# Moving the last group of a modulation map from layer 0's retention stage to layer 1's attention stage

## What is computed

```
for layer 0 and layer 1:
    m = silu(cond) @ w_mod[layer] + b_mod[layer]        # 6 x 1024 columns: shift, scale, gate of two sub-layers
    h = x * (1 + scale) + shift
    layer 0:  out = [latent attention(h), bidirectional retention(h)] @ w_out
    layer 1:  out = windowed attention(h) @ w_out       # 16 heads in 4 groups of keys
    x = LayerNorm(ALPHA * x + gate * out)
    x = LayerNorm(ALPHA * x + gate2 * MoE(x * (1 + scale2) + shift2))   # 64 experts, top 8
```

## Time and profile before

| what | us |
|---|---|
| median of three runs | 1731.41 |
| lowest and highest run | 1728.42, 1732.64 |
| span of the profiled execution | 1731.9 |
| layer 0's retention, start of the block to `product(0, 0)` | 211.8 to 260.7 |
| layer 1's attention, start of the block to the next block's first matmul | 990.3 to 1054.2 |
| PE busy over the span | 1548.0 (89%) |
| DVE, ACT, POOL busy | 587.6, 351.9, 239.1 |
| chain that ended last: PE, DMA, all other engines | 20%, 13%, under 4% |
| moved by DMA | 586.76 MB, mean 339 GB/s |

### The profile page before, as it was taken

How to read it: one execution, slowest core, us unless ns; L and a number is a source line. 1 busy time by engine, 2 the same in 40 slices (tenths; PEclk the granted TensorE clock), 3 DMA queues, 4 the chain that set the end, 5 groups by cost and what they waited for, 6 DMA issues and landing times. The chain is left out here.

```text
span 1731.9 us, 19203 instructions
## 1 busy us (share of the span) xinstructions
PE 1548.0 (89%) x6862; PEld 737.9 (43%) x6862; DVE 587.6 (34%) x1428; ACT 351.9 (20%) x768; POOL 239.1 (14%) x223
## 2 busy tenths in 40 slices
PE   4899889997799899999889889998699899999987
PEld 1566644542344334344334744543244344344332
DVE  2233685532123111111137675632133111111117
ACT  3224621211011111111114272211011111111120
POOL 0010111111011123211100000111011122211100
PEclk9999999998899999999999989998899999999998
DMA  9890389599999999999994116699999999999994
GB/s 383 346 359 34 136 334 360 211 421 421 398 411 420 409 373 410 399 413 420 378 410 154 41 41 246 260 382 420 404 392 420 410 387 395 395 408 413 391 375 172
DMA packets 112498, 586.76 MB, mean 339 GB/s; under 512 B 22154, under 2 KB 24618, under 8 KB 54160
## 3 DMA queue, kind: packets, MB, share of 16 engines
q1 hardware_dynamic: 89264, 533.84, 76.1%
q0 software_dynamic: 22560, 50.00, 7.5%
q10 hardware_dynamic: 576, 1.66, 0.3%
HBM read 570.99 MB, written 45.30 MB: 356 GB/s over the span
## 5 line engine op out<-in xcount | busy, mean ns | idle before, releaser
L3021 DVE TENSOR_TENSOR scratch<-scratch,bank 128x256 f32<-128x256 f32 x84 | 51.5, 613 | 584.7 <-ACT scratch L2989 556.2
L2896 PE MATMUL bank<-weights,scratch 128*64 128x512 f32 x384 | 181.0, 625 | 49.4 <-DMA scratch<-in_moe_w_up 45.4
L2896 PE MATMUL bank<-scratch 128*64 128x512 f32 x352 | 169.1, 636 | 35.1 <-DMA weights<-in_moe_w_up 23.3
L2897 PE MATMUL bank<-scratch 128*64 128x512 f32 x384 | 187.8, 646 | 0.0
L2897 PE MATMUL bank<-weights,scratch 128*64 128x512 f32 x384 | 178.7, 619 | 0.0
L2989 ACT ACTIVATE scratch<-bank 128x256 f32<-128x256 f32 x84 | 32.2, 383 | 643.9 <-PE bank L2897 425.9
L2896 PEld LDWEIGHTS bank<-weights,scratch 128*64 128x64 f32 x384 | 53.4, 144 | 164.1 <-issue 163.9
L2896 PEld LDWEIGHTS bank<-scratch 128*64 128x64 f32 x352 | 50.1, 147 | 143.0 <-issue 142.8
L2626 POOL DMA_INDIRECT y_rows<-hP,y_idx x39 | 41.5, 1063 | 452.6 <-ACT hP L2997 328.7
L2902 PE MATMUL bank<-weights,scratch 128*128 128x512 f32 x224 | 98.5, 593 | 1.7 <-DMA weights<-in_moe_w_up 1.7
L2611 POOL DMA_INDIRECT hP<-h_rows,tok_idx x78 | 81.4, 1043 | 129.1 <-PE bank L2572 61.7
(11 more groups left out here) (402 smaller groups left out, 2405.6 us busy)
## 6 DMA issues: line engine op xcount, KB each, us to landing
weights<-in_moe_w_gate SPq DMA_DIRECT2D x62, 1024.0 KB, 12.9
weights<-in_moe_w_up SPq DMA_DIRECT2D x62, 1024.0 KB, 20.1
weights<-in_moe_w_down SPq DMA_DIRECT2D x62, 1024.0 KB, 20.7
scratch<-in_moe_w_gate SPq DMA_DIRECT2D x60, 1024.0 KB, 12.8
scratch<-in_moe_w_up SPq DMA_DIRECT2D x60, 1024.0 KB, 21.6
scratch<-in_moe_w_down SPq DMA_DIRECT2D x60, 1024.0 KB, 21.4
weights<-in_w_mod SPq DMA_DIRECT2D x6, 2048.0 KB, 11.4
wmod_more<-in_w_mod SPq DMA_DIRECT2D x6, 2048.0 KB, 8.7
```

Of the source, the lines that this page charges most:

```text
L2896: nc.tensor.matmul(out[0:HALF, :], x[:, 0:HALF], w0[:, kk], start=(kk == 0), stop=(kk == KT - 1))
L2897: m = nc.tensor.matmul(out[HALF:P, :], x[:, HALF:P], w1[:, kk], start=(kk == 0), stop=(kk == KT - 1))
L3021: nc.vector.tensor_tensor(B.h[b % 2].rearrange("p (j q) -> p q j", j=2), B.ex[b % 2].rearrange("p (q j) -> p q j", j=2), k.ps[2 + b % 2][: ...
```

## The change

Halves 8 to 15 (group 5) leave layer 0's retention. They become a part of layer 1's attention: one half in each of the steps g = 3 to 10 (`MOD_STEP`), between `scores(g)` and `turns_and_values(g - 2)`, into bank 7. The value sums, which used banks 6 and 7 in turn, now use the two column halves of bank 6. SP gets the loads of the halves (two buffers in the weight ring), the bias loads, the stores of the rows and a wait for them ahead of the fold's loads. In retention the loads shrink to halves 5 to 7, one half is left in each of the first three loop steps, the addition of the bias moves to one place at i = 5, and both `rows_out` calls become one.

```diff
-LATE_LOOP = ((5, 3), (8, 2), (10, 2), (12, 1))
-LATE_LAST = (13, 14, 15)
-LATE_AT = (0, 1, 2, 3, 4, 0, 1, 2, 3, 4, 0, 1, 2, 0, 1, 2)
+LATE_LOOP = (5, 6, 7)
+LATE_AT = (0, 1, 2, 3, 4, 0, 1, 2)
...
+MOD_STEP = 3
-def stage_attention(k, groups, scale, layer, fold_at, ahead=None, beside=None):
+def stage_attention(k, groups, scale, layer, fold_at, ahead=None, beside=None, with_mod=False):
...
+    halves = range(MOD_HALVES, 2 * MOD_HALVES) if with_mod else ()
+    bufs = [k.ring[:, 8192 + i * MOD_COLS:8192 + (i + 1) * MOD_COLS] for i in range(2)]
+    bias, rows = hT[:, 1024:1536], hT[:, 1536:2048]
...
+    def sum_bank(g):
+        return k.ps[6][:, g % 2 * 2 * P:(g % 2 + 1) * 2 * P] if with_mod else k.ps[6 + g % 2][:, 0:2 * P]
...
         def _(sp):
+            def half_in(i):
+                if i >= 2:
+                    sp.wait_ge(s_used, i - 1)
+                sp.dma_start(bufs[i % 2], mod_half(k, halves[i])).then_inc(s_half[i % 2], 16)
+            if with_mod:
+                half_in(0)
+                half_in(1)
+                for r in range(2):
+                    sp.dma_start(bias[r:P:32, :], mod_strips(k.io["b_mod"][mod_layer], mod_c)).then_inc(s_bias, 16)
             if ahead:
                 ahead(sp)
+            if with_mod:
+                for i in range(2, len(halves)):
+                    half_in(i)
+                sp.wait_ge(s_row, 1)
+                for r in range(2):
+                    sp.dma_start(mod_strips(k.mod_d[mod_layer, r], mod_c), rows[r:P:32, :]).then_inc(s_stored, 16)
+                sp.wait_ge(s_stored, 32)
             F.load(k, sp, s_fl, layer, 3, "ln1", layer)
...
+            def mod(i):
+                pe.wait_ge(s_half[i % 2], 16 * (i // 2 + 1))
+                pe_mod_half(k, halves[i], 7, bufs[i % 2]).then_inc(s_used, 1)
             for g in range(G + 2):
                 if g < G:
                     scores(g)
+                if 0 <= g - MOD_STEP < len(halves):
+                    mod(g - MOD_STEP)
                 if g >= 2:
                     turns_and_values(g - 2)
...
+                if with_mod and g == MOD_STEP + MOD_HALVES:
+                    dve.wait_ge(s_used, MOD_HALVES)
+                    dve.wait_ge(s_bias, 32)
+                    nc.vector.tensor_tensor(rows, k.ps[7][:], bias, ALU.add).then_inc(s_row, 1)
```

The DVE part above stands behind `norm(g - 1)` in DVE's loop. In retention, where `HALVES` is now 8, the programs of SP, PE and DVE change so:

```diff
         for n in range(LATE_PLACES, HALVES):
             half_in(n)
-        sp.wait_ge(s_mod, 2 * LATE_PLACES)
+        sp.wait_ge(s_mod, LATE_PLACES)
         out_chunk(k, w_out, 0)(sp)
-        for n in LATE_LAST:
-            half_in(n)
...
-        rows_out(sp, 0)
         sp.wait_ge(s_o, ITEMS)
         sp.wait_ge(s_mod, HALVES)
-    def on_sync_late(sp):
-        rows_out(sp, 1)
+        rows_out(sp)
...
         for i in range(2, ITEMS + 2):
             if i < ITEMS:
                 scores(i)
-                mod(n)
+            if i - 2 < len(LATE_LOOP):
+                mod(LATE_LOOP[i - 2])
             if i <= ITEMS:
                 values(i - 1)
-            if count > 1:
-                mod(n + 1)
             back(i - 2)
-            if count > 2:
-                mod(n + 2)
-        for n in LATE_LAST:
-            mod(n)
...
-            if i == 4:
-                mod_rows(0)
-            if i == ITEMS + 1:
-                mod_rows(1)
+            if i == ITEMS - 1:
+                mod_rows()
...
     stage_attention(k, groups, SD ** -0.5, 2 * o + 1, k.hP[0:16, 0, 0:4 * FoldRows.WIDTH],
-                    both(out_chunk(k, w_out, 0), load_last_norm(k, 2 * o + 1)))
+                    both(out_chunk(k, w_out, 0), load_last_norm(k, 2 * o + 1)), with_mod=True)
```

More of the change, by code:

```diff
@@ L1229, in values @@
                         slice(jj * P, (jj + 1) * P), slice((2 * a + jj) * P, (2 * a + jj + 1) * P))
-                    m = nc.tensor.matmul(k.ps[6 + g % 2][rows, cols], h["v"][2 * jj + a][c], pt[:, x % PT, probs], start=(c == 0), stop=(c == nk - 1))
+                    m = nc.tensor.matmul(sum_bank(g)[rows, cols], h["v"][2 * jj + a][c], pt[:, x % PT, probs], start=(c == 0), stop=(c == nk - 1))
                 return m
@@ L1360, in __init__ @@
         self.DT = hP[:, 0:2 * RH * P].rearrange("p (d h n) -> p d h n", d=2, h=RH)
-        self.bias = hP[:, 2048:3072].rearrange("p (g n) -> p g n", g=2)
+        self.bias = hP[:, 2048:2560]
         self.qdec = hT[:, 0:2 * HP * P].rearrange("p (d h n) -> p d h n", d=2, h=HP)
@@ L1465, in retention_programs, with rows_out @@
     s_mod, s_b, s_row, s_out, s_gated, s_gt, s_cat = sems(nc, ctx, "half_used mod_bias_in mod_rows_ready mod_rows_out gated gated_turned sums_in_place")
-    def rows_out(sp, g):
-        layer, c = mod_group(LATE_GROUPS[g])
-        sp.wait_ge(s_row, g + 1)
+    def rows_out(sp):
+        layer, c = mod_group(LATE_GROUPS[0])
+        sp.wait_ge(s_row, 1)
         for r in range(2):
-            sp.dma_start(mod_strips(k.mod_d[layer, r], c), W.bias[r:P:32, g, :]).then_inc(s_out, 16)
+            sp.dma_start(mod_strips(k.mod_d[layer, r], c), W.bias[r:P:32, :]).then_inc(s_out, 16)
     def on_sync(sp):
@@ L1475, in half_in @@
             sp.dma_start(late[late_place(n)], mod_half(k, n)).then_inc(s_l[late_place(n)], 16)
[L1477 to L1480, removed]
         sp.wait_ge(s_qz, 3)
-        for g in range(2):
-            bias_in(g)
-        for n in range(LATE_PLACES, LATE_LAST[0]):
+        layer, c = mod_group(LATE_GROUPS[0])
+        for r in range(2):
+            sp.dma_start(W.bias[r:P:32, :], mod_strips(io["b_mod"][layer], c)).then_inc(s_b, 16)
+        for n in range(LATE_PLACES, HALVES):
             half_in(n)
-        sp.wait_ge(s_mod, 2 * LATE_PLACES)
+        sp.wait_ge(s_mod, LATE_PLACES)
         out_chunk(k, w_out, 0)(sp)
-        for n in LATE_LAST:
-            half_in(n)
         sp.wait_ge(s_sa, 4)
@@ L1594, in mod @@
                 pe.wait_ge(s_l[late_place(n)], 16 * late_loads(n))
[L1595 removed]
+            pe_mod_half(k, n, MOD_BANK, late[late_place(n)]).then_inc(s_mod, 1)
         for b in range(len(PAIR_JOBS)):
@@ L1747, in gated, with mod_rows @@
             nc.vector.tensor_tensor(out, y, out, ALU.mult).then_inc(s_gated, 1)
-        def mod_rows(g):
-            dve.wait_ge(s_mod, MOD_HALVES * (g + 1))
-            dve.wait_ge(s_b, 64)
-            nc.vector.tensor_tensor(W.bias[:, g], k.ps[MOD_BANK[g]][:], W.bias[:, g], ALU.add).then_inc(s_row, 1)
+        def mod_rows():
+            dve.wait_ge(s_mod, HALVES)
+            dve.wait_ge(s_b, 32)
+            nc.vector.tensor_tensor(W.bias, k.ps[MOD_BANK][:], W.bias, ALU.add).then_inc(s_row, 1)
         for j, (d, t, _) in enumerate(NEW_STATES + CTX_STATES):
```

23 lines of the change are left out of this document (11 added, 12 removed).

## The result

| what | before | after |
|---|---|---|
| median of twelve runs each, on one chip, us | 1731.53 | 1734.91 |
| lowest and highest run | 1727.83, 1734.29 | 1732.39, 1739.63 |
| ratio after to before, 95% interval | | 1.0027, 1.0016 to 1.0039 |
| span of the profiled execution | 1731.9 | 1732.2 |
| retention, first transposition to `product(0, 0)` | 48.95 | 44.78 |

The changed kernel is slower by 0.27%, 4.7 us by the ratio and 3.4 by the medians. The interval lies wholly above 1, so the loss is real, but its middle falls just short of the 0.3% that the prediction took as the least that can be told from no change. The time is inside the range of 1733 to 1746.5, 5 us under the forecast of 1740, and practically at the first rival's 1735.

The account below looks back on a forecast made before the run. PE and the weight stream were taken to bound the kernel in turn. Terms of -4.2 + 0.5 + 9.2 + 1.5 + 1.7 = +8.7 us on the median 1731.4 gave 1740 us, range 1733 to 1746.5.

Parts of the forecast that it names:

- first rival: Attention: SP's chain fits behind PE's last steps, added halves lift the clock early; +3.8 us, 1735; chance 0.20.
- retention's chain to the first product: Layer 0's retention: with eight halves less, DVE sets the pace and the first product starts 4.2 us earlier.
- clock behind the longer wait: Retention's first product: idle time ahead grows to about 6.5 us, so half clock costs 0.5 us more.
- eight halves in attention: Layer 1's attention: halves add 1.00 us each, the first two 1.85 at half clock, 0.5 hidden; +9.2 us.
- tail on SP: End of layer 1's attention: stores, fold loads and folded store end after PE; +1.5 us, bounds 0 and 4.5.
- clock of the next products: Products after layer 1's attention: half clock behind 2.2 us idle instead of 0.73; +1.7 us, bounds 0 and 3.
- The direction: Whole kernel: slower by over 0.3%, given a chance of 0.73.
- second rival: Layer 0's MoE: the weight stream carries time across stages, 8.4 MB less on SP's queue gives -20 us; 1724; chance 0.07.
- the signs: Profile after: among others, attention takes 74 to 76 us from its first matmul to the next block's instead of 63.8.

Follow-up runs that it names:

- attention's part alone: Kernel before with the changed attention on top, all sixteen halves kept in retention, so the last group is made twice; ratio 1.0043, +7.4 us.
- the simpler versions: Kernel after with only halves 13 to 15 left in attention, 0.9987; kernel after with all eight attention halves behind the first transpositions, 0.9989.
- the split one: Kernel after with halves 8 to 12 made in retention's waits and only 13 to 15 in attention's steps 3 to 5; ratio 0.9987, 1729.02 us.
- the whole group with the waits filled: Kernel after with attention's eight halves behind the transpositions, plus seven identity matmuls in retention's waits; ratio 0.9985, 1729.92 us.
- retention's part alone: Kernel after without the halves in attention; the last group's products left out, its rows hold the bias alone; ratio 0.9968, -5.5 us.

## Why the prediction was right, and where it was not

| term | forecast, us | by the trace, us |
|---|---|---|
| retention's chain to the first product | -4.2 | -4.17 |
| clock behind the longer wait | +0.5 | +1.35 |
| eight halves in attention | +9.2 | +5.44 |
| tail on SP | +1.5 | +0.54 |
| clock of the next products | +1.7 | 0 |
| sum | +8.7 | +3.2 |

The timed difference is +4.7 by the ratio, with an interval of 2.8 to 6.8; it holds the trace's sum and not the forecast's.

**The direction** was right, though the size is half of the forecast and falls just short of the 0.3% that it was to exceed. The range held it because it reached down to the first rival, not because the sum came out. The reason was the one given: PE-bound steps took 1.00 us more each (6.41 against 5.41), while retention gave back half of what left it, since DVE became late next. **Retention's chain** is the best term. The replay of DVE's order with the rows' own durations gave 4.2; two kernels show 4.17 and 4.18, and DVE's waits fell as named (0.27 and 0.72, together under 1.5). The idle time ahead of the product was 5.54 us, where 6 to 7 were forecast: `values(5)` ran at half clock and filled a part of it. A transfer of the stage's gain was assumed one to one, and no sign of the second rival's 20 us of stream appeared: between retention and attention 711.04 us passed instead of 712.26, with all of the 8 MB moved.

**The attention term failed**, at the sentence "The first two halves fall in the stretch where PE has half clock (0.50 in the window at 1000), and cost 1.85 each". The stage took 69.80 us, where the signs had named 74 to 76. The first cost 1.59 (1.93 in attention's part alone) and the second 1.06. The prediction then named what it did not count: "If the added work ends the slow stretch one piece earlier, some 1.7 us come back". That is what happened, and it was larger. Full clock came back about 10.3 us behind the stage's first matmul instead of 15.7. Steps 3 to 6 took 20.27 us with four halves, 18.80 without: +1.47, where four halves at full clock are 4.0. Of the missing 2.53 one wait of PE on ACT's copy gives 0.63 (0.96 to 0.33; 0.5 was forecast), the rest, 1.9, is clock. The two identity matmuls in the kernel before show the same without any half: 3.6 us of work for 1.50 us of time. So I held the end of the slow stretch fixed in time, and it is not fixed: it moves with what PE does.

**The tail** was the right path and 1 us too long. The run with the addition moved back shows that the path is live. Its links were 2.27 (2.2 forecast), 3.14 (3.6), 2.56 (2.56) and 2.08 (2.5), so the last two transfer waits were 0.4 us shorter each. The row that I used says 1.9 us from an issue to its landing, and it is of stores that POOL had issued. SP's transfers were quicker, counted from the last issue to what waited for it: 1.68 us behind the second store (1045.39 to 1047.07), 1.43 behind the last load (1048.78 to 1050.21). The first link came out as forecast only because the issues of the two stores lay 0.56 us apart and not 0.3. The Trainium skill, DMA: Bandwidth & Descriptors, section Anatomy of one DMA, gives about 2.0 us as fixed, and tells it of transfers that GpSimd issues. Both of SP's figures here are under it.

**The clock terms** were both mis-sized, in opposite directions. The next products paid nothing, because the idle time was 1.26 us and not the 2.2 that the longer tail would have made; the bound of 3 was right for a longer wait (2.83 behind 5.09). Behind retention's wait the product paid 3.05 us over its 7.13, a little beyond the 2.9 that I had taken as the most. In the profiled executions it took 8.83 to 8.89 behind idle times of 2.38 to 5.90 us and 9.75 to 10.18 in four others, behind 3.70 to 6.67, so 0.5 lay within what one execution may show and 1.35 too.

**The first rival**, "the tail and the clock spare it", gave 1735 and was nearly the result. It was right on attention's clock and on the next products. It was not right that the tail spares it altogether. Its +3.8 against the trace's +3.2 is in part luck: it has no term for the tail (0.54) and 0.5 for the clock behind retention's wait (1.35), and it charges attention 7.5 for 5.44. A chance of 0.20 was too small: its clock part rested on a reading that I had written down myself, and the forecast of 0.55 needed three small penalties to come together.

## What to carry to other kernels

Moving work from a stage that waits to a stage where PE has hardly a wait costs its full length there in every step at full clock, and gives back only what the next engine in line allows; replay that engine's order before moving anything. Inside the PE-bound stage the place matters: ahead of the transpositions a half cost 1.00 us, behind them, where PE waited for ACT's copy, 0.60. A split that puts five of eight halves into waits and three into the slow stretch, with the long wait before the projection filled, had the lowest ratio, 0.9974 (0.9961 to 0.9988). It is faster than the kernel before; its interval overlaps with those of the simpler versions (0.9987 and 0.9989), so that it beats them isn't shown.

## What the hardware showed that was not expected

- The same idle time did not always have the same clock behind it. Behind 2.16 us (2.15 in one) at the same place in retention, eleven kernels went on at 1.00 and two, the split one and the whole group with the waits filled, fell to half for about 3.5 us, which cost 1.6 us each time. `values(5)` ran at half clock behind 1.88 us in the kernel after (0.68 us a matmul group) and not at first behind 1.87 us in retention's part alone (0.44). Ahead of a product, idle times of 0.67 to 1.37 us left full clock in all runs shown here, and 2.38 us and more did not in any.
- PE work in a slow stretch was cheap: 3.6 us of it cost 1.50 us, and four halves of 1.00 us cost 1.47, since the granted clock came back earlier (and, for the halves, one wait shrank by 0.63). In all 13 profiled executions full clock was back 10.3 to 13.5 us behind attention's first matmul where work had been added and 15.1 to 15.7 where none had.
- A float32 matmul of 128x512 with a full 128x128 weight takes 0.86 us at full clock and about 1.8 at half (3.57 us for two of them), so filling a wait needs counting: ten of them took 8.75 us and delayed the product by 1.85.
- What sets whether half clock comes at a given wait stays open; the runs show both outcomes, and in retention PE's rows ahead of the wait of 2.16 us agree to 0.01 us in all 13 executions.
